# RWKV chunks: every second pair of heads changes sides, and four products use four quarters of the array

## Chip, cores and metric

One core of one Trainium2 chip. The metric is the device time of one launch in microseconds (us), the median of the runs.

## The reference, cut to what matters

The kernel computes a two-block model over 512 tokens of width 1024. The change is inside one branch of the first block, RWKV-7: 16 heads of width 64, each with a 64x64 state that is carried over the tokens.

```python
def step(state, inp):
    r_t, w_t, k_t, v_t, kk_t, b_t = inp
    sk = jnp.einsum('bhvk,bhk->bhv', state, kk_t)
    state = (state * w_t[:, :, None, :] - sk[..., None] * b_t[:, :, None, :]
             + v_t[..., None] * k_t[:, :, None, :])
    return state, jnp.einsum('bhvk,bhk->bhv', state, r_t)
```

## The kernel before, in words

The recurrence is run in 8 chunks of 64 tokens. A chunk needs, per head, the inverse of a triangular 64x64 matrix, which is built up by doubling in five levels, and then a few 64x64 products with the state. Two heads make a pair `j` (8 pairs). Head `i=0` of a pair lives in partitions 0 to 63, head `i=1` in partitions 64 to 127. A 64x64 product takes one quarter of the 128x128 array: its rows are the partitions its operands come from, its columns the partitions of PSUM it writes. Before, nearly all products of head 0 go from rows 0-63 to columns 0-63, those of head 1 from rows 64-127 to columns 64-127, so two quarters on the diagonal are used. Only U writes to the other half of the partitions, and so uses the other two quarters.

**prep(c, blk)** inverts for chunk `c` and four pairs (`blk` 0 or 1, 8 heads):
- gram (L758), transposes bt and vt (L767, L771), the first X product (L777). VectorE makes the masked matrices (L2363, L2366), the first `Xi` (L2376) and the first `Xj` (L2379); ScalarE copies NCc (L1546), BT (L1551) and UV (L1557, key vt); GpSimd makes the masks of each level (L3302).
- then for each level `l` = 1 to 5: P (L786) from `Xj`; ScalarE copies it out to `P1` (L1564, key p1); X (L793) and, below level 5, Y (L798) use P1 and `Xi`. VectorE subtracts Y from `Xj` (L2388, key xj), which is what the next P waits for, and then X from `Xi` (L2392, key xi).

**seq(c)** does the part that depends on the state: R (L813 and, from chunk 1, L816), which ScalarE copies to RS (L1431); U (L824), which ScalarE writes negated into UV (L1577, two instructions, key uv); S (L832) and O (L838, L841), with the new state on VectorE (L2405, L2411) and the output on ScalarE (L1582).

`chunk_turns` (L609) sets the order on every engine: seq(c) in three parts, with seven steps of prep(c+1) for the two blocks in turn after the first and after the second part, and the rest of prep(c+1) behind. In steady state TensorE's order is: R; gram, bt, vt and first X of both blocks; PA(1) (A is block 0, B is block 1, in brackets stands the level); U; PB(1); XA YA XB YB of level 1; PA(2) PB(2) XA YA XB YB of level 2; S and O; PA(3) PB(3) XA YA XB YB; the same for level 4; PA PB XA XB of level 5; R of the next chunk.

PSUM results come from a ring of seven banks (`PS`, class `Ring`). `take` hands out the next bank, and `bank` makes TensorE wait until the bank's previous owner was read out (`prior`). Order and waits on an engine are in program order: what stands behind a wait waits too.

```python
def bank(*key, hold=False):
    b = PS.take(*key, hold=hold)
    for s in due("pe", *PS.prior(*key)):
        pe.wait_ge(*s)
    return b
```

Of the kernel before, what the change touches and what calls it, by code (L numbers as in the profile page):

```python
# [16 lines left out]
S = 512  # L17
# [155 lines left out]
class Ring:  # L173
# [10 lines left out]
    def take(self, *key, hold=False):  # L184
        while self.n % len(self.slots) in self.held:
            self.n += 1
        i = self.n % len(self.slots)
        self.n += 1
        assert key not in self.at, key
        self.at[key], self.before[key], self.owner[i] = i, self.owner[i], key  # L190
        if hold:
            self.held.add(i)
        return self.slots[i]

    def let(self, *key):
        self.held.discard(self.at[key])
# [3 lines left out]

    def prior(self, *key):

        k = self.before[key]
        if k is None:
            return self.after
        return [] if self.known is None else self.known[1][k]

    def free(self, key, *done):
        assert key not in self.freed, key
# [115 lines left out]
def build(nc, T, known=None):  # L325

    with ExitStack() as ctx:
# [36 lines left out]
            return list(zip(tiles(sb(c, name + "h", n * S, dt=F32R)), tiles(sb(c, name + "l", n * S, dt=F32R))))  # L364


        PS = ring("ps", [ctx.enter_context(nc.psum_tensor("ps%d" % i, [128, S], F32))[:, :] for i in range(7)])
        PL = ctx.enter_context(nc.psum_tensor("psl", [128, S], F32))[:, :]
        PT, CT, DP, X = sb(ctx, "PT", NPAR), sb(ctx, "CT", NCON), sb(ctx, "DP", 76), sb(ctx, "X", 8 * S)
        W = Weights(T, sb(ctx, "wraw", NRAW * SLOT), sb(ctx, "whi", NSPL * SLOT, dt=F32R),  # L370
# [138 lines left out]

        halves = [(i, 64 * i, slice(64 * i, 64 * i + 64)) for i in range(2)]  # L510
        each = [(j, i, lo, sl) for j in range(8) for i, lo, sl in halves]
        o3 = YS.rearrange("p (j t) -> p j t", j=8)
        xw, rt, rec, Lc, Pp, Pi, at_, km = Yt

# [105 lines left out]
        def tensor_program(pe):  # L620

            def bank(*key, hold=False):
                b = PS.take(*key, hold=hold)
                for s in due("pe", *PS.prior(*key)):
                    pe.wait_ge(*s)
                return b

            def proj(b, key, w, rhs, hk, c0=0, m=128, start=True, stop=True, k0=0, ks=None):

# [117 lines left out]
            def prep(c, blk):  # L747
                u = c % 2
                cols = slice(256 * blk, 256 * blk + 256)
                xi3, xj3, p13 = (r3(a[:, cols], 64) for a in (Xis[u], Xj, P1))  # L750
                nls = [r3(x[:, cols], 64) for x in NLr]
                mine = [(jj, i, lo, sl) for jj in range(4) for i, lo, sl in halves]
                for s in due("pe", ("dve", "bk", 4 * blk + 3), ("act", "kr", 4 * blk + 3)):
                    pe.wait_ge(*s)
                gram = [r3(bank("gram", c, blk, i), 128) for i in range(2)]
                for jj, i, lo, sl in mine:
                    j = 4 * blk + jj
                    ins = MM(gram[i][:, jj, :], BK5[sl, j, c, :, :].rearrange("p s t -> p (s t)"),  # L758
                             KR5[sl, j, c, :, :].rearrange("p s t -> p (s t)"), start=True, stop=True)
                    if jj == 3:  # L760
                        ins.then_inc(*up("pe", "gram", c, blk, i))
                if c == 0 and blk == 1:
                    rk_sum(7)
                yield
                b3 = r3(bank("bt", c, blk), 128)
                for jj in range(4):
                    ins = TR(b3[:, jj, :], BK5[:, 4 * blk + jj, c, :, :].rearrange("p s t -> p (s t)"), C("ident"))  # L767
                ins.then_inc(*up("pe", "bt", c, blk))
                b3 = r3(bank("vt", c, blk), 128)
                for jj in range(4):  # L770
                    ins = TR(b3[:, jj, :], VFt[4 * blk + jj][:, c // 2 * 128:c // 2 * 128 + 128], C("ident"))  # L771
                ins.then_inc(*up("pe", "vt", c, blk))
                b3 = r3(bank("x", c, blk, 0)[:, 0:256], 64)
                for s in due("pe", ("dve", "lvl", c, blk, 0)):
                    pe.wait_ge(*s)
                for jj, i, lo, sl in mine:
                    ins = MM(b3[sl, jj, :], nls[0][sl, jj, :], C("x0")[sl, :], start=True, stop=True)  # L777
                ins.then_inc(*up("pe", "x", c, blk, 0))
                yield
                yield  # L780
                for l in range(1, 6):
                    b3 = r3(bank("p", c, blk, l)[:, 0:256], 64)
                    for s in due("pe", ("dve", "xj", c, blk, l - 1), ("pool", "lvl", c, blk, l)):
                        pe.wait_ge(*s)
                    for jj, i, lo, sl in mine:
                        ins = MM(b3[sl, jj, :], nls[l % 3][sl, jj, :], xj3[sl, jj, :], start=True, stop=True)  # L786
                    ins.then_inc(*up("pe", "p", c, blk, l))
                    yield
                    b3 = r3(bank("x", c, blk, l)[:, 0:256], 64)
                    for s in due("pe", ("act", "p1", c, blk, l), ("dve", "xi", c, blk, l - 1)):  # L790
                        pe.wait_ge(*s)
                    for jj, i, lo, sl in mine:
                        ins = MM(b3[sl, jj, :], p13[sl, jj, :], xi3[sl, jj, :], start=True, stop=True)  # L793
                    ins.then_inc(*up("pe", "x", c, blk, l))
                    if l < 5:
                        b3 = r3(bank("y", c, blk, l)[:, 0:256], 64)
                        for jj, i, lo, sl in mine:
                            ins = MM(b3[sl, jj, :], xi3[sl, jj, :], p13[sl, jj, :], start=True, stop=True)  # L798
                        ins.then_inc(*up("pe", "y", c, blk, l))
                    yield  # L800


            def seq(c):
                u = c % 2
                GT, BT, UV = GTs[u], BTs[u], UVs[u]
                xi3, rs3, st3 = r3(Xis[u], 64), r3(RS, 64), r3(ST, 64)
                b3 = r3(bank("R", c), 64)
                for blk in range(2):
                    for s in due("pe", ("dve", "gt", c, blk, 1), ("act", "vt", c, blk, 1), ("act", "bt", c, blk),
                                 ("dve", "xi", c, blk, 5), ("dve", "st", c - 1) if c else None):  # L810
                        pe.wait_ge(*s)
                for j, i, lo, sl in each:
                    ins = MM(b3[sl, j, :], GT[sl, j, i, 0:64], UV[sl, j, i, :], start=(j == 0), stop=(c == 0 and j == 7))  # L813
                if c:
                    for j, i, lo, sl in each:
                        ins = MM(b3[sl, j, :], KR5[sl, j, c, 0, :], st3[sl, j, :], start=False, stop=(j == 7))  # L816
                ins.then_inc(*up("pe", "R", c))
                yield
                b3 = r3(bank("U", c), 64)
                for s in due("pe", ("act", "rs", c)):  # L820
                    pe.wait_ge(*s)
                for j, i, lo, sl in each:
                    ul = slice(64 - lo, 128 - lo)
                    ins = MM(b3[ul, j, :], xi3[sl, j, :], rs3[sl, j, :], start=True, stop=True)  # L824
                ins.then_inc(*up("pe", "U", c))
                yield
                if c < 7:
# [585 lines left out]
        def scalar_program(act):  # L1413
# [118 lines left out]
            def prep(c, blk):  # L1532
# [28 lines left out]
                for l in range(1, 6):  # L1561
                    for need in due("act", ("pe", "p", c, blk, l)):
                        act.wait_ge(*need)
                    ACTV(P1[:, cols], PS.of("p", c, blk, l)[:, 0:256], ACT.Copy).then_inc(*up("act", "p1", c, blk, l))  # L1564
                    PS.free(("p", c, blk, l), ("act", "p1", c, blk, l))
                    yield
                    yield

            def seq(c):
                evac(("R", c), RS, ACT.Copy, ("rs", c))  # L1570
                yield
                b3 = r3(PS.of("U", c), 64)
                for need in due("act", ("pe", "U", c)):
                    act.wait_ge(*need)
                for i, lo, sl in halves:
                    ul = slice(64 - lo, 128 - lo)
                    ACTV(UVs[c % 2][ul, :, i, :], b3[ul, :, :], ACT.Copy, scale=-1.0).then_inc(*up("act", "uv", c, i))  # L1577
                PS.free(("U", c), ("act", "uv", c, 1))
                yield
                for need in due("act", ("pe", "O", c)):  # L1580
                    act.wait_ge(*need)
                ACTV(o3[:, :, c * 64:(c + 1) * 64], r3(PS.of("O", c), 64), ACT.Copy).then_inc(*up("act", "o", c))  # L1582
                PS.free(("O", c), ("act", "o", c))
# [571 lines left out]
        def vector_program(dve):  # L2155
# [196 lines left out]
            def prep(c, blk):  # L2352
# [20 lines left out]
                yield  # L2373
                for need in due("dve", ("dve", "lvl", c, blk, 0)):
                    dve.wait_ge(*need)
                TT(xi3, bmid(C("x0"), 4), nl3, SUB).then_inc(*up("dve", "xi", c, blk, 0))  # L2376
                for need in due("dve", ("pe", "x", c, blk, 0), ("pe", "p", c - 1, blk, 5) if c else None):
                    dve.wait_ge(*need)
                TT(xj3, bmid(C("x0"), 4), r3(PS.of("x", c, blk, 0)[:, 0:256], 64),  # L2379
# [3 lines left out]
                for l in range(1, 6):  # L2383
                    yield
                    if l < 5:
                        for need in due("dve", ("pe", "y", c, blk, l), ("dve", "xj", c, blk, l - 1)):
                            dve.wait_ge(*need)
                        TT(Xjb, Xjb, PS.of("y", c, blk, l)[:, 0:256], SUB).then_inc(*up("dve", "xj", c, blk, l))  # L2388
                        PS.free(("y", c, blk, l), ("dve", "xj", c, blk, l))
                    for need in due("dve", ("pe", "x", c, blk, l), ("dve", "xi", c, blk, l - 1)):  # L2390
                        dve.wait_ge(*need)
# [1118 lines left out]
```

## Time and profile before

| | |
|---|---|
| median of 3 runs | 3808.95 us (3808.34 to 3809.26) |
| the profiled execution | 3807.86 us, of which the span is 3806.1 us |
| TensorE busy in the span | 3685.7 us (97%) |
| VectorE, ScalarE busy | 2143.5 us (56%), 1490.1 us (39%) |
| mean granted TensorE clock | 0.984 of 2.4 GHz |
| the chunk stage | about 199.6 to 425 us of the span |

Times in rows are microseconds from the start of the span. TensorE's matmul records are PE, its weight loads PEld. One 64x64 fp32 product shows as two matmul records: the 8 products of P for one block are "x16". A row of the timeline gives start, length from first start to last end, engine, line, operation and count; in square brackets stands how long the engine had been idle and what ended that.

### The profile page before, as it was taken

Reading aid. Unit: us, or ns where it says so; the run is one execution under the profiler, and the core shown is the slowest. Engines: PE = TensorE matmul, PEld = TensorE weight load, DVE = VectorE, ACT = ScalarE, POOL = GpSimd, SP = SyncE. Lnnn points to the kernel's source line nnn. Section 1 sums busy time; section 2 is a strip of 40 time slices with the busy share of each in tenths; the row PEclk is TensorE's granted clock in tenths of the full one; section 3 lists DMA queues with packets and bytes.
Section 4 is the critical chain, followed back from the end, with each engine's and each line's share of the span. In section 5 each row is a group of like instructions: output and inputs, shape, how many; then the busy total and the mean of one; then the engine's idle time right before and its main releaser. Section 6 shows DMA issues by size and latency. Waiting matters only on the chain.

```text
span 3806.1 us, 51932 instructions
## 1 busy us (share of the span) xinstructions
PE 3685.7 (97%) x22058; PEld 2987.6 (78%) x22058; DVE 2143.5 (56%) x3227; ACT 1490.1 (39%) x2593; POOL 72.2 (2%) x92
## 2 busy tenths in 40 slices
PE   8989999899999999999999999999999999999998
PEld 6678688787876887887777888888877778888886
DVE  6865645757444466567575445434665654454346
ACT  5733334335222344343355323223434562332233
POOL 0022000000000000000000000000000000000000
PEclk9999999899999999999999999999999999999999
DMA  3200123022331222323200223232332003332322
GB/s 140 66 3 4 57 89 105 23 100 72 101 115 50 89 95 90 104 89 110 81 1 21 82 95 110 89 106 85 98 107 68 1 23 100 102 105 86 108 87 81
DMA packets 91532, 298.57 MB, mean 78 GB/s; under 512 B 10147, under 2 KB 12707, under 8 KB 90788
## 3 DMA queue, kind: packets, MB, share of 16 engines
q1 hardware_dynamic: 88848, 286.50, 23.2%
q10 hardware_dynamic: 2452, 8.76, 0.6%
q8 instruction: 173, 2.83, 0.3%
q14 instruction: 59, 0.48, 0.0%
HBM read 292.07 MB, written 2.10 MB: 77 GB/s over the span
## 4 chain that ended last, share of the span: by engine, by line
PE 85%; DVE 9%; ACT 4%; issue 1%; DMA 0%; SPq 0%; DVEq 0%; POOL 0%; ACTq 0%; POOLq 0%
PE ps L638 22%; PE ps L640 22%; PE ps L639 22%; PE ps L1264 2%; PE ps L1274 1%; PE psl L1283 1%; DVE wlo L2161 1%; PE ps L1283 1%; ACT whi L1421 1%; PE ps L793 1%; PE ps L677 1%; DVE ftm L2177 1%; PE ps L679 1%; PE ps L678 1%; PE ps L798 1%
## 5 line engine op out<-in xcount | busy, mean ns | idle before, releaser
L2161 DVE TENSOR_TENSOR wlo<-wraw,whi 128x1024 fp32r<-128x1024 f32 (+5 forms) x603 | 663.5, 1102 | 1212.8 <-ACT whi L1421 1203.6
L1421 ACT ACTIVATE whi<-wraw 128x1024 fp32r<-128x1024 f32 (+5 forms) x603 | 576.1, 958 | 1195.3 <-PE ps L640 1117.8
L638 PE MATMUL ps<-HH,whi 128*128 128x512 f32 x1880 | 749.1, 398 | 9.8 <-DVE wlo L2161 7.3
L640 PE MATMUL ps<-HH,wlo 128*128 128x512 f32 x1880 | 733.2, 390 | 0.0
L639 PE MATMUL ps<-HL,whi 128*128 128x512 f32 x1880 | 733.1, 390 | 0.0
L638 PEld LDWEIGHTS ps<-HH,whi 128*128 128x128 f32 x1880 | 353.8, 188 | 98.1 <-issue 12.7
L639 PEld LDWEIGHTS ps<-HL,whi 128*128 128x128 f32 x1880 | 353.9, 188 | 78.8 <-issue 7.5
L640 PEld LDWEIGHTS ps<-HH,wlo 128*128 128x128 f32 x1880 | 353.6, 188 | 74.3
L638 PE MATMUL ps<-HBh,whi 128*128 128x512 f32 x816 | 320.9, 393 | 1.4 <-DVE HBl L2779 0.9
L640 PE MATMUL ps<-HBh,wlo 128*128 128x512 f32 x816 | 317.7, 389 | 0.0
L639 PE MATMUL ps<-HBl,whi 128*128 128x512 f32 x816 | 317.6, 389 | 0.0
L638 PEld LDWEIGHTS ps<-HBh,whi 128*128 128x128 f32 x816 | 153.2, 188 | 35.8 <-DVE HBl L2779 2.1
L639 PEld LDWEIGHTS ps<-HBl,whi 128*128 128x128 f32 x816 | 153.2, 188 | 32.5 <-issue 1.4
L640 PEld LDWEIGHTS ps<-HBh,wlo 128*128 128x128 f32 x816 | 153.2, 188 | 31.9
L638 PE MATMUL ps<-act2h,whi 128*128 128x512 f32 x384 | 149.8, 390 | 0.0
L639 PE MATMUL ps<-act2l,whi 128*128 128x512 f32 x384 | 149.4, 389 | 0.0
L640 PE MATMUL ps<-act2h,wlo 128*128 128x512 f32 x384 | 149.4, 389 | 0.0
L3063 DVE TENSOR_REDUCE sm<-ps 128x1 f32<-128x256 f32 (+3 forms) x192 | 81.2, 451 | 55.5 <-PE ps L1266 55.2
L638 PE MATMUL ps<-yph,whi 128*128 128x512 f32 x256 | 100.2, 391 | 0.7 <-DVE ypl L2170 0.7
L639 PE MATMUL ps<-ypl,whi 128*128 128x512 f32 x256 | 99.6, 389 | 0.0
L640 PE MATMUL ps<-yph,wlo 128*128 128x512 f32 x256 | 99.6, 389 | 0.0
L638 PEld LDWEIGHTS ps<-act2h,whi 128*128 128x128 f32 x384 | 72.1, 188 | 15.8 <-DVE act2l L2170 1.0
(648 smaller groups left out, 6093.5 us busy)
## 6 DMA issues: line engine op xcount, KB each, us to landing
wraw<-in_w_ff SPq DMA_DIRECT2D x88, 512.0 KB, 3.4
wraw<-in_w_bg SPq DMA_DIRECT2D x48, 512.0 KB, 3.4
wraw<-in_ffn_up SPq DMA_DIRECT2D x44, 512.0 KB, 3.2
wraw<-in_w_z SPq DMA_DIRECT2D x36, 512.0 KB, 3.2
wraw<-in_w_gate SPq DMA_DIRECT2D x32, 512.0 KB, 3.3
wraw<-in_w_br SPq DMA_DIRECT2D x32, 512.0 KB, 3.2
wraw<-in_w_rw SPq DMA_DIRECT2D x26, 512.0 KB, 3.3
wraw<-in_w_mam SPq DMA_DIRECT2D x24, 512.0 KB, 3.2
```

What stands on the lines that cost most here:

```text
L638: MM(b[0:m, :], hi[:, k, c0:c0 + m], x[0], start=(start and k == 0), stop=False)
L639: MM(b[0:m, :], hi[:, k, c0:c0 + m], x[1], start=False, stop=False)
L640: ins = MM(b[0:m, :], lo[:, k, c0:c0 + m], x[0], start=False, stop=(stop and k == n - 1))
L677: MM(b[:, 0:cols], x[0][:, cs], hi[:, k, 0:cols], start=first, stop=False)
L678: MM(b[:, 0:cols], x[1][:, cs], hi[:, k, 0:cols], start=False, stop=False)
L679: ins = MM(b[:, 0:cols], x[0][:, cs], lo[:, k, 0:cols], start=False, stop=end)
L793: ins = MM(b3[sl, jj, :], p13[sl, jj, :], xi3[sl, jj, :], start=True, stop=True)
L1264: MM(b[h][:, 0:nk], job["q"](h)[:, qs], job["k"](h)[:, k0:k0 + nk], start=True, stop=False)
L1283: ins = MM(ob[:, 64 * h:64 * h + 64], job["pt"][i % 3][:, 128 * kb:128 * kb + 128], job["v"](h, kb), start=(kb == 0), stop=(kb == nkb - 1))
L1421: ACTV(W.pair_of(n)[0], W.raw_of(n), ACT.Copy).then_inc(*up("act", "whi", n))
L2161: TT(l, W.raw_of(n), h.bitcast(F32), SUB).then_inc(*up("dve", "wlo", n))
L3063: RED(s[:, h:h + 1], PS.of("sc", *key)[:, 0:job["nk"]], AXX, ALU.max, negate=True).then_inc(*(up("dve") if x else up("dve", "mx", *key)))
```

## The change

Every odd pair of heads changes sides on its way. `turned(j, lo)` gives the other half for odd `j`. P of an odd pair is written to the opposite half of PSUM, so that `P1` of that pair lies in the other half; `Xi` of odd pairs lies in the other half too, which the first `Xi` brings about: one VectorE instruction over 128x256 becomes one over 128x128 and two over 64x128. X then reads and writes in the other half (still on the diagonal), Y, R and U go between halves as needed. P, Y, R and U thus use all four quarters, and write even pairs to one bank and odd pairs to another: each takes two neighbouring banks. `Ring.take_two` hands out banks 0-1, 2-3 or 4-5, passing over a bank where it stands on an odd one or on the last (number 6). X, S, O, gram and the transposes take one bank as before; the seven banks stay seven. ScalarE's and VectorE's reads of the four products go over both banks in one instruction.

```diff
+    def take_two(self, *key):
+        n = len(self.slots)
+        while self.n % n % 2 or self.n % n == n - 1 or {self.n % n, self.n % n + 1} & self.held:
+            self.n += 1
+        i = self.n % n
+        self.n += 2
+        assert key not in self.at, key
+        self.at[key], self.before[key] = i, self.owner[i:i + 2]
+        self.owner[i:i + 2] = [key, key]
+        return self.slots[i:i + 2]
...
-        k = self.before[key]
-        if k is None:
-            return self.after
-        return [] if self.known is None else self.known[1][k]
+        done = []
+        for k in self.before[key]:
+            if k is None:
+                done += self.after
+            elif self.known is not None:
+                done += self.known[1][k]
+        return done
...
-        PS = ring("ps", [ctx.enter_context(nc.psum_tensor("ps%d" % i, [128, S], F32))[:, :] for i in range(7)])
+        PSW = [ctx.enter_context(nc.psum_tensor("ps%d" % i, [128, 2 * S if i < 3 else S], F32))[:, :] for i in range(4)]
+        PS = ring("ps", [b for w in PSW for b in tiles(w)])
+
+        def two(key, n):
+
+            w = PSW[PS.at.get(key, 0) // 2 if known is None else known["rings"]["ps"][0][key] // 2]
+            return w.rearrange("p (e n) -> p e n", e=2)[:, :, 0:64 * n].rearrange("p e (a t) -> p e a t", a=n)
+
+        def by_two(ap):
+            return ap.rearrange("p (a e) t -> p e a t", e=2)
...
+        def turned(j, lo):
+            lo = 64 - lo if j % 2 else lo
+            return slice(lo, lo + 64)
...
+            def two_banks(*key):
+
+                banks = [r3(b, 64) for b in PS.take_two(*key)]
+                for s in due("pe", *PS.prior(*key)):
+                    pe.wait_ge(*s)
+                return banks
...
-                    b3 = r3(bank("p", c, blk, l)[:, 0:256], 64)
+                    bb = two_banks("p", c, blk, l)
                     for s in due("pe", ("dve", "xj", c, blk, l - 1), ("pool", "lvl", c, blk, l)):
                         pe.wait_ge(*s)
                     for jj, i, lo, sl in mine:
-                        ins = MM(b3[sl, jj, :], nls[l % 3][sl, jj, :], xj3[sl, jj, :], start=True, stop=True)
+                        ins = MM(bb[jj % 2][turned(jj, lo), jj // 2, :], nls[l % 3][sl, jj, :], xj3[sl, jj, :],
+                                 start=True, stop=True)
                     ins.then_inc(*up("pe", "p", c, blk, l))
                     yield
                     b3 = r3(bank("x", c, blk, l)[:, 0:256], 64)
                     for s in due("pe", ("act", "p1", c, blk, l), ("dve", "xi", c, blk, l - 1)):
                         pe.wait_ge(*s)
                     for jj, i, lo, sl in mine:
-                        ins = MM(b3[sl, jj, :], p13[sl, jj, :], xi3[sl, jj, :], start=True, stop=True)
+                        tl = turned(jj, lo)
+                        ins = MM(b3[tl, jj, :], p13[tl, jj, :], xi3[tl, jj, :], start=True, stop=True)
                     ins.then_inc(*up("pe", "x", c, blk, l))
                     if l < 5:
-                        b3 = r3(bank("y", c, blk, l)[:, 0:256], 64)
+                        bb = two_banks("y", c, blk, l)
                         for jj, i, lo, sl in mine:
-                            ins = MM(b3[sl, jj, :], xi3[sl, jj, :], p13[sl, jj, :], start=True, stop=True)
+                            tl = turned(jj, lo)
+                            ins = MM(bb[jj % 2][sl, jj // 2, :], xi3[tl, jj, :], p13[tl, jj, :], start=True, stop=True)
                         ins.then_inc(*up("pe", "y", c, blk, l))
...
-                b3 = r3(bank("R", c), 64)
+                bb = two_banks("R", c)
                 for blk in range(2):
                     for s in due("pe", ("dve", "gt", c, blk, 1), ("act", "vt", c, blk, 1), ("act", "bt", c, blk),
                                  ("dve", "xi", c, blk, 5), ("dve", "st", c - 1) if c else None):
                         pe.wait_ge(*s)
                 for j, i, lo, sl in each:
-                    ins = MM(b3[sl, j, :], GT[sl, j, i, 0:64], UV[sl, j, i, :], start=(j == 0), stop=(c == 0 and j == 7))
+                    ins = MM(bb[j % 2][turned(j, lo), j // 2, :], GT[sl, j, i, 0:64], UV[sl, j, i, :], start=(j < 2),
+                             stop=(c == 0 and j > 5))
                 if c:
                     for j, i, lo, sl in each:
-                        ins = MM(b3[sl, j, :], KR5[sl, j, c, 0, :], st3[sl, j, :], start=False, stop=(j == 7))
+                        ins = MM(bb[j % 2][turned(j, lo), j // 2, :], KR5[sl, j, c, 0, :], st3[sl, j, :], start=False,
+                                 stop=(j > 5))
                 ins.then_inc(*up("pe", "R", c))
                 yield
-                b3 = r3(bank("U", c), 64)
+                bb = two_banks("U", c)
                 for s in due("pe", ("act", "rs", c)):
                     pe.wait_ge(*s)
                 for j, i, lo, sl in each:
-                    ul = slice(64 - lo, 128 - lo)
-                    ins = MM(b3[ul, j, :], xi3[sl, j, :], rs3[sl, j, :], start=True, stop=True)
+                    ul, tl = slice(64 - lo, 128 - lo), turned(j, lo)
+                    ins = MM(bb[j % 2][ul, j // 2, :], xi3[tl, j, :], rs3[tl, j, :], start=True, stop=True)
                 ins.then_inc(*up("pe", "U", c))
...
-                    ACTV(P1[:, cols], PS.of("p", c, blk, l)[:, 0:256], ACT.Copy).then_inc(*up("act", "p1", c, blk, l))
+                    ACTV(by_two(r3(P1[:, cols], 64)), two(("p", c, blk, l), 2), ACT.Copy).then_inc(*up("act", "p1", c, blk, l))
...
-                    ACTV(UVs[c % 2][ul, :, i, :], b3[ul, :, :], ACT.Copy, scale=-1.0).then_inc(*up("act", "uv", c, i))
+                    ACTV(by_two(UVs[c % 2][:, :, i, :])[ul], b4[ul], ACT.Copy, scale=-1.0).then_inc(*up("act", "uv", c, i))
...
-                TT(xi3, bmid(C("x0"), 4), nl3, SUB).then_inc(*up("dve", "xi", c, blk, 0))
+                TT(xi3[:, 0::2, :], bmid(C("x0"), 2), nl3[:, 0::2, :], SUB)
+                for i, l_, sl in halves:
+                    ins = TT(xi3[turned(1, l_), 1::2, :], bmid(C("x0")[sl, :], 2), nl3[sl, 1::2, :], SUB)
+                ins.then_inc(*up("dve", "xi", c, blk, 0))
...
-                        TT(Xjb, Xjb, PS.of("y", c, blk, l)[:, 0:256], SUB).then_inc(*up("dve", "xj", c, blk, l))
+                        TT(by_two(xj3), by_two(xj3), two(("y", c, blk, l), 2), SUB).then_inc(*up("dve", "xj", c, blk, l))
```

## Rows read from the trace of the kernel before

**Rows 1.** Windows of the chunk stage: stretch, its length, busy time (and records) by engine, clock, DMA.
```profile
195.00:420.00 225.00, 203.20 (x5586) 186.90 (x5586) 120.92 (x264) 80.55 (x193) 57.56 (x80) 0.98 0.03 8
```

**Rows 2.** Groups by line in that stage: busy us, mean ns | idle before.
```profile
L793 PE MATMUL ps<-Xi,P 64*64 64x64 f32 x1280 | 51.8, 220 | 2.5 <-ACT P L1564 2.1
...
L786 PE MATMUL ps<-Xj,NL 64*64 64x64 f32 x1280 | 51.5, 221 | 2.3 <-POOL NL L3302 0.3 <-DVE Xj L2388 0.2
...
L798 PE MATMUL ps<-P,Xi 64*64 64x64 f32 x1024 | 40.5, 218 | 0.0
...
L813 PE MATMUL ps<-UV,X 64*64 64x64 f32 x256 | 9.2, 220 | 4.9 <-DVE Xi L2392 4.9
...
L824 PE MATMUL ps<-RSs,Xi 64*64 64x64 f32 x256 | 9.2, 221 | 0.7 <-ACT RSs L1431 0.7
...
L816 PE MATMUL ps<-ST,KR 64*64 64x64 f32 x224 | 7.9, 218 | 0.0
```

**Rows 3.** Timeline of one chunk, where its four stretches begin.
```profile
249.03 1.15 PE L813 MATMUL ps<-UV,X 64*64 64x64 f32 x32 [0.61 <-DVE Xi L2392]
...
257.38 0.51 PE L786 MATMUL ps<-Xj,NL 64*64 64x64 f32 x10
...
267.54 1.10 PE L786 MATMUL ps<-Xj,NL 64*64 64x64 f32 x32
...
276.82 1.15 PE L813 MATMUL ps<-UV,X 64*64 64x64 f32 x32 [0.62 <-DVE Xi L2392]
```

**Rows 4.** Timeline of one level, from P of level 4 to P of level 5.
```profile
270.60 1.37 PE L786 MATMUL ps<-Xj,NL 64*64 64x64 f32 x32
...
271.15 0.41 DVE L2392 TENSOR_TENSOR Xi<-Xi,ps 128x256 f32<-128x256 f32 x1
...
271.28 0.38 ACT L1564 ACTIVATE P<-ps 128x256 f32<-128x256 f32 x1 [2.20 <-PE ps L786]
...
271.80 0.63 PE L793 MATMUL ps<-Xi,P 64*64 64x64 f32 x16
...
273.67 1.37 PE L786 MATMUL ps<-Xj,NL 64*64 64x64 f32 x32
```

**Rows 5.** Chain that ended last, same level.
```profile
270.81 0.43 DVE Xj L2388
...
271.24 0.04 issue
```

**Rows 6.** Timeline where P and U stand beside each other.
```profile
257.68 0.27 PE L824 MATMUL ps<-RSs,Xi 64*64 64x64 f32 x2
...
257.69 0.28 PE L786 MATMUL ps<-Xj,NL 64*64 64x64 f32 x3
...
258.50 0.27 PE L786 MATMUL ps<-Xj,NL 64*64 64x64 f32 x2
...
258.54 0.28 PE L824 MATMUL ps<-RSs,Xi 64*64 64x64 f32 x3
```

**Rows 7.** Timeline of VectorE and ScalarE around the first P.
```profile
256.53 0.42 DVE L2376 TENSOR_TENSOR Xi<-CT,NL 128x256 f32<-128x256 f32 x1
...
257.20 0.91 DVE L2376 TENSOR_TENSOR Xi<-CT,NL 128x256 f32<-128x256 f32 x1
...
257.55 0.77 ACT L1557 ACTIVATE UV<-ps 64x256 f32<-64x256 f32 x2
...
258.87 1.21 ACT L1577 ACTIVATE UV<-ps 64x512 f32<-64x512 f32 x2
```

**Rows 8.** Windows with the granted clock, and one row at the lower clock.
```profile
255.00:258.00 3.00, 2.06 (x49) 1.71 (x49) 2.97 (x6) 2.76 (x8) 2.21 (x4) 1.00 0.00 0
...
415.00:420.00 5.00, 3.54 (x108) 3.15 (x102) 0.50 (x2) 0.71 (x2) 0.00 (x0) 1.00 0.00 0
...
420.00:425.00 5.00, 3.72 (x64) 3.47 (x64) 0.00 (x0) 1.15 (x3) 0.00 (x0) 0.66 0.01 3
...
421.15 1.97 PE L838 MATMUL ps<-X,UV 128*64 128x64 f32 x32 [1.31 <-ACT UV L1577]
```

More of the change, by code:

```diff
@@ L189, in take @@
         assert key not in self.at, key
-        self.at[key], self.before[key], self.owner[i] = i, self.owner[i], key
+        self.at[key], self.before[key], self.owner[i] = i, [self.owner[i]], key
         if hold:
@@ L1569, in seq @@
             def seq(c):
-                evac(("R", c), RS, ACT.Copy, ("rs", c))
+                for need in due("act", ("pe", "R", c)):
+                    act.wait_ge(*need)
+                ACTV(by_two(r3(RS, 64)), two(("R", c), 4), ACT.Copy).then_inc(*up("act", "rs", c))
+                PS.free(("R", c), ("act", "rs", c))
                 yield
-                b3 = r3(PS.of("U", c), 64)
+                b4 = two(("U", c), 4)
                 for need in due("act", ("pe", "U", c)):
```

## The prediction

> **What bounds the kernel now.** I read the windows first: over the chunk stage TensorE is busy 203 of 225 us, VectorE 121, ScalarE 81, at nearly the full clock [rows 1]. TensorE looks like the bound. The groups say what fills it: P, X and Y in 3584 records, R and U in 736 [rows 2]. Then the timeline of one level. XA, YA, XB, YB start at 271.80 and the next P at 273.67 [rows 4]: 64 records in 1.87 us, so 29.2 ns from record to record, while one record lasts 220 ns [rows 2]; records overlap, and it is the rate that counts. A level takes 273.67 - 270.60 = 3.07 us [rows 4], of which 96 records at 29.2 ns make 2.80. The rest is PB waiting for its `Xj`: YB is through at 270.60, VectorE starts at 270.81, so 0.21 later, takes 0.43, and 0.04 of issue follow before PB at 271.28 [rows 4, 5]. The copy of PA starts as far behind it: PA's 16 records are through at 271.07, the copy starts at 271.28 and takes 0.38 [rows 4]; the 0.05 behind a copy I take like the 0.04 behind VectorE. So behind the busy share stand two chains, one per block, nearly as long as the work: P, 0.21, copy 0.38, 0.05, X, Y, 0.21, xj 0.43, 0.04. (A and B are blocks 0 and 1; a number in brackets is the level.)
>
> **What four quarters free.** With two quarters, each takes a record every 58 ns. With four, one every 14.6 ns in all, if the streams don't hinder each other. No single product does that now, but two do side by side: U uses the other two quarters, and where it meets P both run at their own pace: three records of P in 0.28 and three of U in 0.28 [rows 6], less the 0.22 of one record 0.06 for two steps, 30 ns each. P of block 1 starts at 258.50 while records of U, which stand ahead of it in the program, start at 258.54 [rows 6]. So the array takes records of other quarters past waiting ones. I take 14.6 ns; the other end is 29.2. A rule speaks against this: the Trainium skill, "TensorE: Matmul & The Clock Gate", section "The mechanism", says that matmuls start and end strictly in program order. By that rule the sum would be that of the second rival below; the trace of P and U disagrees with it.
> P 1280 records, Y 1024, R 480 and U 256 [rows 2] save 3040 x 14.6 ns = 44 us of TensorE's work. How much of it comes through, I work out by the four stretches of a cycle [rows 3], which is 27.79 us long (276.82 - 249.03).
>
> **What takes it back: the banks.** A level took 6 banks out of 7; now it takes 10, and pairs only at even places. Writing the ring out gives this, the same in every chunk from level 3 on: PA [0,1], PB [2,3] or PA [2,3], PB [4,5]; XA in 4 or 6, YA [0,1], XB in 2, YB [4,5]. Three waits are new and bind. YB of levels 2 and 4 takes the bank of XA of the same level, which is free only after VectorE's xj and xi of block 0. PB of levels 2, 4 and 5 takes the bank of XB of the level before, so it waits for xi of block 1 and not only for xj. U takes the banks of bt and vt of block 1, so it waits for ScalarE's vt. Behind each of them waits all of TensorE's queue: behind YB the next PA, behind PB the next XA, though the copy of PA is long there, behind U the PB of level 1.
> In the walks below, each time is that of the latest thing waited for. 16 records take 0.47 on two quarters and 0.23 on four; a reader starts 0.21 after the last of them was issued; from the start of xj to that of xi are 0.34, xi takes 0.41, a copy 0.38 [rows 4, 5], and 0.05 pass before TensorE goes on.
>
> **Stretch 1, R to gram.** 64 records at half the step: -0.93. Nothing covers it: gram, and behind it VectorE, follow at once.
> **Stretch 2, gram to PA(1).** VectorE sets the pace here, and the first Xi becomes three instructions. One of 256 columns takes 0.42 [rows 7] and lets the next start 0.34 later. If the step scaled with width, three of 128 would take 0.51 (+0.17); if not at all, 1.02 (+0.68). On ScalarE a 256-wide copy takes 0.38 [rows 4] and a 512-wide one 0.60 [rows 7], so some 0.16 doesn't scale; with that I take 0.62: +0.28. The same for block 1, where the row shows 0.91 beside GpSimd [rows 7], falls where TensorE waits for ScalarE (next) and costs nothing; without that cover +0.3 to +0.6.
> **Stretch 3, PA(1) to PA(3),** 10.16 before [rows 3]. From PA(1): vt ends at 258.32 [rows 7], now 0.66 after PA; U 0.71 to 1.18, uv (1.21 for two [rows 7]) 1.39 to 2.60, the copy of PB to 2.90, XB 2.95, YB to 3.65, PA(2) to 3.88, xj 3.86, xi 4.20 to 4.61, PB(2) 4.66 to 4.89, XA to 5.36, YA to 5.59, XB to 6.06; YB waits: xj 5.80, xi 6.14 to 6.55; YB 6.60 to 6.83. S and O are unchanged, 96 records of 29.2 ns and some 0.2 where the shape of the products changes: 3.0. PA(3) at 9.8: -0.34.
> **Stretch 4, PA(3) to R,** 9.28 before. ScalarE copies O first, so XA(3) starts at 0.21 + 0.60 + 0.38 + 0.05, less some 0.1 for the overlap of two copies: 1.14, as before, since P is over by then either way; YB ends at 2.54; PA(4); xj 2.75, xi 3.09 to 3.50; PB(4) 3.55, XA 3.78, YA to 4.48; xj 4.69, xi 5.03 to 5.44; YB 5.49, PA(5) to 5.95; xi of block 1 to 6.69, PB(5) 6.73, XA 6.97; XB 7.61 to 8.08, xi to 8.71, R 8.85: -0.43. With no bank waits it would be 1.2 less.
> ScalarE's and VectorE's reads over two banks I cost at nothing (same elements, one instruction); SyncE's loads of x behind O of chunks 6 and 7 keep their place, the weight loads are far ahead.
>
> **Sum.** A full cycle: -0.93 + 0.28 - 0.34 - 0.43 = -1.42, seven of them -9.9. The preparation of chunk 0 has both waits at every level: 3.19 for 3.07 four times, and Xi: +0.8. R of chunk 0 is half as long: +0.5. The last R and U: -0.9 and -0.5. In all -10.0 of the 44 freed. Against the profiled execution's 3807.86 that is 3797.9; the median lies 1.1 above it: 3799.
>
> **Rivals.**
> *The clock falls.* Less work per time means more idle stretches. Where TensorE was busy 2.06 of 3.00 us the clock stayed at 2.4 GHz; after 3.54 of 5.00, most of the idle time in its second half, it was at 1.2 for part of the next stretch (0.66 in the mean) [rows 8]. Around PA(1) it will be busy some 1.9 of 3.4 (the same stretch with 0.3 more to wait and with PA and U shorter, an estimate), between the two. At 1.2 GHz 32 records took 1.97 [rows 8], so (1.97 - 0.27)/31 = 55 ns each, not 29; with chains beside it, 1.0 to 1.7 us per fall of 3.4 us. Once per chunk: 3807 to 3812. Chance 0.14.
> *No four-quarter rate within one product.* Each product is two records on the same quarter, and if the second holds up what follows, two records per 58 ns stay, as now. This is the case on the other side; its place is YB and PB behind the new bank waits. Per cycle: YB of levels 2 and 4 +0.54 each (xi ends 1.90 after XA's start, XB at 1.40), PB of levels 2, 4 and 5 +0.33 each, U's wait +0.36, Xi +0.28: +2.7, times seven and 3.8 for chunk 0: +23, 3832. On a line between -10 at 14.6 ns and +23 at 29.2 the gain is gone at a step of 19 ns, and from 22 ns on it is slower by over 0.2%. For it: the two records. Against it: rows 6. Chance 0.12. By the Trainium skill's rule of program order ("TensorE: Matmul & The Clock Gate", "The mechanism") this would be the outcome.
> *The waits bind less,* because read-outs come sooner than I chain them. Without any of them a cycle gains the 1.2 of stretch 4 and 0.9 in stretch 3 (PB(2) 0.33, YB(2) 0.54): 2.1, times seven, 3784. Against it: each length is from a row. Chance 0.08.
> *The change doesn't do what it says:* X keeps two quarters, as the diff says; nothing else in it can fail quietly.
>
> **Numbers.** My forecast, 3799 with its own range 3794 to 3807 (step 14.6 to 17 ns, Xi +0.17 to +0.68 a chunk), has 0.66. Range over all: 3788 to 3813, leaving out most of the second and third rival. 0.2%, 7.6 us, is about what can be told from no change: faster means under 3801.3. From the forecast 0.46 of its 0.66 lies there, with the third rival 0.54; within 0.2%: 0.20 and 0.09 of the clock's case, 0.29; slower 0.17.
>
> **What would show it.** P and Y of 16 records should last about 0.45 in place of 0.63, R's 64 about 1.15, at an unchanged 218 ns per record. TensorE's busy time should fall far more than the span, and idle time stand ahead of L793, L798 and L786 with VectorE's L2392 as what ended it. Xi of the first level shows three instructions. Levels 3.07 long should become 2.3 to 3.2, in turns. The granted clock in the stage should stay at 0.98. Wrong: P of 16 still at 0.63 (no four quarters), a clock under 0.95 in the stage, or a cycle under 26 or over 27.

## The result, and the profile after

The change makes the kernel slower: 3817.5 us against 3809.0, medians of 11 runs each, ratio 1.0024 with an interval of 1.0016 to 1.0031. 3799 was predicted. The profiled execution took 3814.36 us with a span of 3812.6, 6.5 longer than before. The runs further down were measured at other times, and each is compared with the kernel before as measured beside it (medians of 3807.4 to 3810.1), so differences between runs are best read from their ratios.

First the windows of the chunk stage after the change (stretch, length, busy time and records of TensorE, weight loads, VectorE, ScalarE, GpSimd; granted clock, DMA):

```profile
215.00:400.00 185.00, 142.31 (x4624) 127.87 (x4624) 102.72 (x233) 63.37 (x151) 43.38 (x60) 0.95 0.01 3
290.00:295.00 5.00, 3.70 (x105) 3.52 (x108) 2.26 (x6) 1.95 (x4) 2.79 (x5) 0.66 0.01 3
318.00:322.00 4.00, 3.50 (x106) 3.31 (x108) 1.83 (x6) 1.83 (x4) 3.07 (x5) 0.57 0.02 6
376.00:384.00 8.00, 6.56 (x196) 6.10 (x187) 3.27 (x9) 2.72 (x6) 3.93 (x6) 0.57 0.02 4
```

In the same 185 us before, TensorE was busy 170.3 us at a clock of 1.00. Now it is 142.3 at 0.95, and the clock is at its lower level (1.2 GHz) for a part of five of the six full cycles. Each such drop and return is called a fall below. The groups answer to [rows 2]:

```profile
L831 PE MATMUL ps<-Xi,P 64*64 64x64 f32 x1280 | 56.4, 231 | 4.4 <-ACT P L1605 4.0
...
L822 PE MATMUL ps<-Xj,NL 64*64 64x64 f32 x1280 | 37.6, 237 | 28.9 <-DVE Xi L2439 14.8 <-DVE Xj L2426 11.5 <-issue 1.9
L837 PE MATMUL ps<-P,Xi 64*64 64x64 f32 x1024 | 34.8, 240 | 7.0 <-DVE Xi L2439 7.0
...
L2422 DVE TENSOR_TENSOR Xi<-CT,NL 64x128 f32<-64x128 f32 x32 | 16.9, 528 | 0.4
```

P is busy 37.6 us where it was 51.5, but TensorE now stands idle 28.9 us ahead of it, where it was 2.3. Two things end that idle time: the read-out of X (L2439), which frees a bank, and the first Xj (L2426). The timeline of a level answers to [rows 4]; it runs from PB(4) to PB(5):

```profile
275.02 0.46 PE L822 MATMUL ps<-Xj,NL 64*64 64x64 f32 x16 [0.57 <-DVE Xi L2439]
275.30 0.57 PE L831 MATMUL ps<-Xi,P 64*64 64x64 f32 x14
...
276.00 0.67 PE L831 MATMUL ps<-Xi,P 64*64 64x64 f32 x16
276.25 0.42 DVE L2435 TENSOR_TENSOR Xj<-Xj,ps 128x256 f32<-128x256 f32 x1 [1.28 <-PE ps L837]
276.59 0.41 DVE L2439 TENSOR_TENSOR Xi<-Xi,ps 128x256 f32<-128x256 f32 x1
277.06 0.46 PE L837 MATMUL ps<-P,Xi 64*64 64x64 f32 x16 [0.39 <-DVE Xi L2439]
277.34 0.41 PE L822 MATMUL ps<-Xj,NL 64*64 64x64 f32 x16
277.59 0.42 DVE L2435 TENSOR_TENSOR Xj<-Xj,ps 128x256 f32<-128x256 f32 x1 [0.58 <-PE ps L837]
...
277.92 0.42 DVE L2439 TENSOR_TENSOR Xi<-Xi,ps 128x256 f32<-128x256 f32 x1
278.40 0.46 PE L822 MATMUL ps<-Xj,NL 64*64 64x64 f32 x16 [0.64 <-DVE Xi L2439]
```

P and Y of 16 records take 0.46 in place of 0.63, for which this is a row of the kernel before:

```profile
259.48 0.63 PE L798 MATMUL ps<-P,Xi 64*64 64x64 f32 x16
```

So four quarters work at the full rate. The waits stand where they were written out: YB(4) at 277.06 and PB(5) at 278.40, each behind an `Xi` update. The first P of a chunk is the other place (before in [rows 7]):

```profile
259.31 0.28 DVE L2420 TENSOR_TENSOR Xi<-CT,NL 128x128 f32<-128x128 f32 x1
...
259.60 1.14 DVE L2422 TENSOR_TENSOR Xi<-CT,NL 64x128 f32<-64x128 f32 x2
...
260.78 0.42 DVE L2426 TENSOR_TENSOR Xj<-CT,ps 128x256 f32<-128x256 f32 x1
261.12 0.37 DVE L2420 TENSOR_TENSOR Xi<-CT,NL 128x128 f32<-128x128 f32 x1
261.25 0.46 PE L822 MATMUL ps<-Xj,NL 64*64 64x64 f32 x16 [1.24 <-DVE Xj L2426]
261.49 1.02 DVE L2422 TENSOR_TENSOR Xi<-CT,NL 64x128 f32<-64x128 f32 x2
...
262.55 0.42 DVE L2426 TENSOR_TENSOR Xj<-CT,ps 128x256 f32<-128x256 f32 x1
263.02 0.46 PE L822 MATMUL ps<-Xj,NL 64*64 64x64 f32 x16 [0.84 <-DVE Xj L2426]
```

The three instructions of Xi take 1.47 us from start to Xj's start, where one took 0.34, and TensorE waits 1.24 for PA(1) and 0.84 for PB(1). Chunks 4 and 6 are like this one. In chunks 3, 5 and 7 the three for block 0 take 0.91 and those for block 1 take 1.86 (before, the one took 0.33 for block 0 and 0.83 to 0.87 for block 1).

The table takes the starts of R, PA(1), PA(3) and the next R from each kernel's timeline, for the six full cycles (from chunk 1 on), and sums from the first P to the last R of the stage. It is the ruler for all that follows.

| us | R to PA(1) | PA(1) to PA(3) | PA(3) to R | cycle | first P to R of chunk 0 | R of chunk 0 to R of chunk 7 |
|---|---|---|---|---|---|---|
| before | 8.35 | 10.16-10.22 | 9.28 | 27.8 | 15.9 | 193.2 |
| change | 7.97-8.53 | 9.94-12.00 | 9.47 | 27.9-30.0 | 18.1 | 200.5 |
| e1 bank plan | 7.97-8.60 | 9.55-11.25 | 8.37-9.09 | 25.9-28.2 | 14.9 | 188.1 |
| e2 Xj first | 7.06-7.17 | 10.80-10.87 | 9.47-9.72 | 27.3-27.6 | 17.1 | 192.2 |
| e3 banks alone | 8.30 | 11.91-12.08 | 10.62-10.76 | 30.8-31.0 | 19.7 | 215.1 |
| e4 Xi in three | 8.83 | 10.70 | 9.28 | 28.8 | 18.6 | 200.2 |
| e5 plan, Xj first | 7.06-7.17 | 9.64-10.85 | 8.37-9.09 | 25.2-26.7 | 14.7 | 180.5 |
| e9 GpSimd waits | 7.97 | 9.93-11.11 | 9.47-9.72 | 27.4-28.7 | 17.5 | 193.7 |

The 6.5 us of the span come out as +2.3 before R of chunk 0, +7.3 in the seven cycles, +0.7 ahead of the first P, and -3.7 from the last R to the end: R and U are shorter there, and the clock, low at L838 before [rows 8], stays up.

### The profile page after: what moved, and what is told of

Same layout as the page of the kernel before. It is cut to its first block, busy times and chain, and to the rows that moved or that the text cites. A ratio compares the mean times of both kernels' runs of the same rounds, so it can differ in the third digit from the quotient of the medians.

```text
span 3812.6 us, 51930 instructions
## 1 busy us (share of the span) xinstructions
PE 3655.9 (96%) x22058; PEld 2953.9 (77%) x22058; DVE 2157.4 (57%) x3259; ACT 1490.0 (39%) x2593; POOL 72.5 (2%) x92
## 4 chain that ended last, share of the span: by engine, by line
PE 83%; DVE 12%; ACT 4%; issue 2%; DMA 0%; SPq 0%; DVEq 0%; ACTq 0%
PE ps L674 22%; PE ps L676 22%; PE ps L675 22%; PE ps L1305 2%; DVE wlo L2205 2%; PE ps L1315 1%; PE psl L1324 1%; ACT whi L1462 1%; PE ps L1324 1%; PE ps L713 1%; DVE ftm L2221 1%; PE ps L715 1%; PE ps L714 1%; PE ps L831 1%; PE ps L1236 1%
## 5 line engine op out<-in xcount | busy, mean ns | idle before, releaser
L674 PEld LDWEIGHTS ps<-act2h,whi 128*128 128x128 f32 x384 | 72.1, 188 | 15.9 <-DVE act2l L2214 0.9
```

What stands on the lines that cost most here:

```text
L674: MM(b[0:m, :], hi[:, k, c0:c0 + m], x[0], start=(start and k == 0), stop=False)
```

## The experiments

**e1, a bank plan in place of the ring.** No P, X or Y waits for a bank any more: PA and YA in banks 0-1, PB and YB in 2-3, X in 4 and 5 (6 at level 3). `place` records the previous owners as `take_two` does; all seven banks now belong to one PSUM tensor.

```diff
+        def spot(kind, c, blk=0, l=0):
+            if kind == "gram":
+                return 2 + 2 * blk + l
+            if kind in ("bt", "vt"):
+                return {"bt": (6, 2), "vt": (0, 3)}[kind][blk]
+            if kind == "x":
+                return (1, 4)[blk] if l == 0 else (6 if l == 3 else 4, 5)[blk]
+            if kind in ("p", "y"):
+                return 2 * blk
+            return {"R": 0, "U": 5, "S": 6, "O": 4}[kind]
...
-                banks = [r3(b, 64) for b in PS.take_two(*key)]
+                banks = [r3(b, 64) for b in PS.place(spot(*key), 2, *key)]
```

> The changed kernel with a bank plan written out in place of the ring: P and Y of block 0 always in banks 0-1, of block 1 in 2-3, X in 4 and 5 (6 at level 3), U in 5-6, so that no P, X or Y waits for a bank. If the bank waits are what takes the gain back, levels go from 3.35 and 2.80 us to about 2.3, the stretch from P of level 3 to R from 9.47 to about 8.3, and the time falls by 15 to 20 us to 3797 to 3802 (less if the clock falls more often, as the stage gets emptier). If the waits are only another face of the chain of copies, levels stay over 3 us and the time within 3 us of 3817.

Measured: 3801.1 us, ratio to the kernel before 0.9984 (0.9974 to 0.9993). The levels of chunk 0 take 2.47 to 2.52 where they took 3.37; PA(3) to R is 8.37 in most cycles, 8.3 expected. What a P waits for is now its own Xj, and shorter:

```profile
288.01 0.46 PE L844 MATMUL ps<-Xj,NL 64*64 64x64 f32 x16 [0.31 <-DVE Xj L2457]
```

The first P of block 1 is put down to ScalarE's UV in the list of waits (7 times), but it starts 0.10 us behind the end of its Xj in all seven, so that its wait too is for its input. The clock still falls (mean 0.95 from 215 to 400 us), once each in two full cycles, of 28.1 and 28.2 against 25.9 to 27.2. The change lies 8.6 us over the kernel before, this one 6.5 under it: the bank waits are a cause, worth 15 us of time.

**e3, the banks without the gain.** The two-bank ring with no head turned and Xi in one instruction: `turned` returns the same half, all else as in the change.

```diff
         def turned(j, lo):
-            lo = 64 - lo if j % 2 else lo
             return slice(lo, lo + 64)
...
-                TT(xi3[:, 0::2, :], bmid(C("x0"), 2), nl3[:, 0::2, :], SUB)
-                for i, l_, sl in halves:
-                    ins = TT(xi3[turned(1, l_), 1::2, :], bmid(C("x0")[sl, :], 2), nl3[sl, 1::2, :], SUB)
-                ins.then_inc(*up("dve", "xi", c, blk, 0))
+                TT(xi3, bmid(C("x0"), 4), nl3, SUB).then_inc(*up("dve", "xi", c, blk, 0))
```

> The kernel with two banks for each P, Y, R and U and the same ring of seven as in the change, but with no head turned: two quarters as before, the first Xi in one instruction. If the array's rate and the banks are separate terms, this pays for the banks without the gain: levels of 3.1 to 4.0 us, 20 us over the kernel before, about 3829. If the waits are hidden at the slower rate, 3809.

Measured: 3834.1 us, ratio 1.0072 (1.0057 to 1.0087).

```profile
332.70 0.68 PE L821 MATMUL ps<-Xj,NL 64*64 64x64 f32 x16 [0.38 <-DVE Xi L2435]
...
335.17 0.68 PE L836 MATMUL ps<-P,Xi 64*64 64x64 f32 x16 [0.39 <-DVE Xi L2435]
```

P and Y last 0.68 and wait for the same two read-outs as in the change. Pairs of banks in a ring of seven cost 26 us by themselves (25 by the two profiled spans), with the clock at 1.00 from 215 to 400 us.

**e4, Xi in three, alone.** The kernel before with three instructions, on the same halves:

```diff
-                TT(xi3, bmid(C("x0"), 4), nl3, SUB).then_inc(*up("dve", "xi", c, blk, 0))
+                TT(xi3[:, 0::2, :], bmid(C("x0"), 2), nl3[:, 0::2, :], SUB)
+                for i, l_, sl in halves:
+                    ins = TT(xi3[sl, 1::2, :], bmid(C("x0")[sl, :], 2), nl3[sl, 1::2, :], SUB)
+                ins.then_inc(*up("dve", "xi", c, blk, 0))
```

> The kernel before with only the first Xi in three instructions (same halves). If three instructions beside GpSimd are what holds up the first P, it comes 0.5 to 1.1 us later in each chunk; some of it hides under ScalarE's copies of U, so the time rises by 2 to 8 us, to 3811 to 3817. The clock should not fall in the stage except at its end, since the rest of the stage is as full as before. If the pieces cost what their width says, under 2 us.

Measured: 3816.1 us, ratio 1.0024 (1.0015 to 1.0034), as much as the whole change costs. Every cycle is 1.0 longer, half of it ahead of PA(1), half behind it. The second part I had taken to be hidden under ScalarE's copies of U. It isn't: PB(1) waits for its Xj, and XA behind PB. The profiled execution is one of the longer ones (3818.2), and in it the clock fell once in chunk 0 (near 210 us), which I had not expected; so a part of the 8.5 us can be the clock's.

**e9, GpSimd kept away from Xi.** The change, with one wait more on GpSimd:

```diff
+                if blk:
+                    for need in due("pool", ("dve", "xi", c, blk, 0)):
+                        pool.wait_ge(*need)
                 level(1)
                 level(2)
```

> The changed kernel with GpSimd made to wait, ahead of its level masks of block 1, until the first Xi of block 1 is made, so that these three VectorE instructions have no GpSimd work beside them. If GpSimd beside them is what stretches them, each takes 0.28 us and the three some 0.7 to 0.85 in a row (0.37 and 1.0 to 1.45 in the change), and Xj of block 1 comes sooner. If they are long for their shape, they stay over 1.3. The first P of block 1 then waits for its mask, 0.75 us, so the time moves little, 3814 to 3820.

Measured: 3810.7 us, ratio 1.0001 (0.9992 to 1.0011), better than expected. Groups of lines of this kernel:

```profile
L2422 DVE TENSOR_TENSOR Xi<-CT,NL 64x128 f32<-64x128 f32 x32 | 9.6, 300 | 0.4
L2420 DVE TENSOR_TENSOR Xi<-CT,NL 128x128 f32<-128x128 f32 x16 | 4.6, 290 | 0.0
```

In the change the first of these groups took 528 ns in the mean, here 300. So it is GpSimd's masks beside them, not the shape, that stretch the instructions. The excess over the kernel before went from 8.6 us to 0.6, so that one added wait took 8 us off. More than half of it is the clock's: between R of chunk 0 and R of chunk 7 a single fall is left where the change had five, one of them twice as long as the others, and full cycles without a fall take 27.4 to 27.6, against 27.9 in the change. The Trainium skill, "SBUF — State Buffer", section "Who interferes with whom", says that a VectorE instruction with two inputs in SBUF contends with a GpSimd instruction that reads SBUF. The trace agrees: Xi has both inputs in SBUF; Xj (L2426), which reads one from PSUM, takes 422 ns in the change and 410 before.

**e2, Xj ahead of Xi.** The change, with the Xj block moved ahead of the three instructions; P needs only Xj.

```diff
-                TT(xi3[:, 0::2, :], bmid(C("x0"), 2), nl3[:, 0::2, :], SUB)
-                for i, l_, sl in halves:
-                    ins = TT(xi3[turned(1, l_), 1::2, :], bmid(C("x0")[sl, :], 2), nl3[sl, 1::2, :], SUB)
-                ins.then_inc(*up("dve", "xi", c, blk, 0))
                 for need in due("dve", ("pe", "x", c, blk, 0), ("pe", "p", c - 1, blk, 5) if c else None):
                     dve.wait_ge(*need)
                 TT(xj3, bmid(C("x0"), 4), r3(PS.of("x", c, blk, 0)[:, 0:256], 64),
                    SUB).then_inc(*up("dve", "xj", c, blk, 0))
                 PS.free(("x", c, blk, 0), ("dve", "xj", c, blk, 0))
+                TT(xi3[:, 0::2, :], bmid(C("x0"), 2), nl3[:, 0::2, :], SUB)
+                for i, l_, sl in halves:
+                    ins = TT(xi3[turned(1, l_), 1::2, :], bmid(C("x0")[sl, :], 2), nl3[sl, 1::2, :], SUB)
+                ins.then_inc(*up("dve", "xi", c, blk, 0))
```

> The changed kernel with one move: the first Xj is made ahead of the three instructions for the first Xi. If these stand in the way of the first P, the first P comes 0.5 to 1.1 us sooner in a chunk for block 0 and about 2 us sooner for block 1, X of level 1 is then held by Xi or by ScalarE, and the time falls by 4 to 10 us. If Xi is hidden, nothing changes.

Measured: 3806.5 us, ratio 1.0000 (0.9991 to 1.0009), 9 to 10 us less than the change when each is held against its kernel before, the top of the expected gain. PA(1) comes 0.8 to 1.5 us sooner after R than in the change. The next wait shows the third bank wait of the prediction, U behind ScalarE's vt:

```profile
314.97 0.69 PE L865 MATMUL ps<-RSs,Xi 64*64 64x64 f32 x32 [0.89 <-ACT UV L1598]
```

In the six full cycles the clock stays up here, and all of them lie between 27.3 and 27.6. So, as in e9, a good part of the gain lies in falls that are gone and not in the shorter wait itself.

**e8, the same order in the kernel before.**

```diff
-                TT(xi3, bmid(C("x0"), 4), nl3, SUB).then_inc(*up("dve", "xi", c, blk, 0))
...
                 PS.free(("x", c, blk, 0), ("dve", "xj", c, blk, 0))
+                TT(xi3, bmid(C("x0"), 4), nl3, SUB).then_inc(*up("dve", "xi", c, blk, 0))
```

> The kernel before with only the first Xj ahead of the first Xi. The first P comes 0.3 us sooner; if nothing else holds it, the time is 2 to 3 us shorter (3805 to 3807), which would be within what a measurement tells from no change. If the gain of the last two runs comes from this order and not from the four quarters, it is 8 us or more.

Measured: 3807.3 us, ratio 0.9998 (0.9990 to 1.0007): no difference. PA(1) is 0.15 to 0.3 sooner after R, and PA(3) 0.17 later behind it. So the order is worth nothing in the kernel before, where Xi is one instruction, and the gain of e2 is not one of the order alone.

**e7, filler products against the fall of the clock.** In the change, 12 products on the spare bank behind the first X of block 1 and 12 behind U.

```diff
+            def fill(n):
+                for s in due("pe", ("dve", "bs")):
+                    pe.wait_ge(*s)
+                for k in range(n):
+                    sl = slice(64 * (k % 2), 64 * (k % 2) + 64)
+                    ins = MM(PL[sl, 0:64], C("x0")[sl, :], C("x0")[sl, :], start=True, stop=True)
+                ins.then_inc(*up("pe"))
...
                 ins.then_inc(*up("pe", "x", c, blk, 0))
+                if c and blk == 1:
+                    fill(12)
...
                 ins.then_inc(*up("pe", "U", c))
+                if c < 7:
+                    fill(12)
```

> The changed kernel with 12 filler products behind the first X of block 1 and 12 behind U, in TensorE's idle time; nobody reads them. If the falls of the clock cost some 7 us in the stage, the clock stays at its upper level between 203 and 420 us, the stretch from the first P to P of level 3 is 9.9 us in every chunk (it is 9.94 to 12.0), and the time is 3809 to 3812. If the long stretches have another cause, they stay with the clock up, at 3817.

Measured: 3812.5 us, ratio 1.0013 (1.0004 to 1.0022), against 1.0024 for the change; the two intervals overlap. The clock stays up from 219 to 420 us, and the seven cycles take 197.4 in place of 200.5. But two of them are long with the clock up (28.4 and 28.5; PA(1) to PA(3) takes 9.9 to 11.1, not 9.9 in every chunk as expected), so that the fillers get in the way somewhere, or something else stretches these; and the clock falls in chunk 0 and once near 423. The profiled execution is also the longest of the ten, 3819.6. The run speaks for the clock without settling its size. Better are the kernels in which single cycles differ by a fall: in e9 five cycles take 27.4 to 27.6, and the one with a fall in it 28.7; in e2, without any, all are alike. A fall costs 1.1 to 1.2 us. Two rows of windows, 215 to 400 us, of e2 and then of the filler run:

```profile
215.00:400.00 185.00, 143.32 (x4748) 127.85 (x4750) 111.13 (x246) 68.47 (x164) 46.82 (x67) 0.99 0.01 3
```

```profile
215.00:400.00 185.00, 148.75 (x4983) 134.25 (x4984) 104.19 (x236) 63.97 (x152) 44.38 (x62) 0.99 0.02 4
```

TensorE is busy hardly more in e2 than in the change (143.3 and 142.3), and the clock still holds. What differs between the two is the idle time ahead of PA(1) and PB(1), which is shorter in e2; the kernels don't show more than that of the cause of a fall.

**e5 and e11, plan and order together.** The edits of e1 and e2 in one kernel, run in two jobs.

> The bank plan and the first Xj ahead of Xi together. If the two were separate terms of the loss, the cycle of a chunk gets under 26 us (from 27.9 to 30.0), levels of chunk 0 stay at 2.5, and the time comes to 3788 to 3795. If the gain of one only opens the wait of the other, it stays near the 3801 of the bank plan alone.

> The bank plan and Xj ahead of Xi once more, beside the run before it on the same chip: 3787 to 3792.

Measured: 3790.3 us, ratio 0.9955 (0.9942 to 0.9969), and again 3792.1, ratio 0.9959 (0.9945 to 0.9972). This beats both kernels, by 17 and 27 us. The full cycles take 25.2 to 26.7 in e5, so not all are under 26 as expected. What P (L844) waits for in e5, by the list of waits:

```profile
PE ps L844 <- DVE Xj L2444: 8.8, 7, 1.3
PE ps L844 <- DVE Xj L2457: 6.6, 23, 0.7
```

No wait for an Xi update is left among the P and Y (14.8 and 7.0 us in the change); the two that remain are the true inputs of P.

**e6, the same with 8 fillers behind U.** `fill` as in e7, in e5:

```diff
                 ins.then_inc(*up("pe", "U", c))
+                if c < 7:
+                    fill(8)
```

> The same with 8 filler products behind U, whose results nobody reads, in TensorE's idle time. If the clock falls in the run without them, it stays up here, and the time is 1 to 2 us per saved fall shorter; if no fall is there to save, the two are the same within 3 us.

Measured: 3794.2 us, ratio 0.9960 (0.9948 to 0.9973), the same as without. In the profile the clock stays up all through the stage and the seven cycles take 178.3 in place of 180.5, but that doesn't show in the medians; the profiled execution, 3788.3, is the fastest of its five.

**e10, all three.** The kernel of e5 with the wait of e9, the same three lines ahead of `level(1)`.

> The bank plan, the first Xj ahead of Xi, and GpSimd's wait together. If the three are separate terms, this is the fastest: 3783 to 3789, with cycles of 25 us or less. If GpSimd's wait only moves the mask of block 1 into the chain that Xj has just left, it is no faster than the two alone (3790), or up to 4 us slower.

Measured: 3801.3 us, ratio 0.9980 (0.9971 to 0.9989), so 9 us worse than e11, the same without GpSimd's wait in the same job, and outside both expectations. Once Xj has left the queue behind Xi, the mask of block 1 is what PB(1) waits for (PA(1) to PA(2) takes 4.5 to 4.6 with the clock up, 4.1 to 4.2 in e11), and the clock falls in three of the full cycles (26.9 to 27.3 against 25.7 to 26.1):

```profile
PE ps L844 <- POOL NL L3371: 9.5, 5, 2.1
```

## Why the prediction was wrong

- **The rate of four quarters: right.** 16 records last 0.46, and R took 1.09 in place of 2.01 up to gram: -0.92 for -0.93 predicted. TensorE's busy time fell by 30 us over the span. "No four-quarter rate" fell; as a price of the banks its sum was some 5 us short: +23 computed, of which 2 for Xi, against +26 measured in e3. That 3832 and 3834 lie so near each other is luck, as the kernel before was 1.4 us faster beside e3 and Xi is not in it.
- **The bank waits: right in place, a little short in size.** YB(2), YB(4) and PB(2), PB(4), PB(5) wait as written out. The third wait, U behind ScalarE's vt, hardly bound in the change (its weight loads waited 1.1 us for it in all), as PA(1) came late itself; it shows in e2. Stretch 4 came to 9.47 and not 8.85. PA(3) to PA(4) took 2.80 (2.54), PA(4) to PA(5) 3.35 (3.18), the rest 3.32 (3.13). Two sizes were off: a run of products that starts after a wait goes slower at its start (P is followed by X 0.28 after it began, not 0.23), and XA(3) starts 1.34 behind PA(3), not 1.14. A tenth of that is only the boundary: PA(3) starts ahead of O's last records now. Stretch 3 was -0.22 with the clock up, for -0.34.
- **Xi in three: this step failed.** "I take 0.62: +0.28", with +0.68 as the far end, priced three instructions without GpSimd, and held block 1 for hidden. Alone each piece starts 0.30 after the one before it, so 0.9 for three, since a 64x128 piece takes as long as a 128x128 one (0.28); beside GpSimd it took 1.47 in the rows above. Stretches 1 and 2 came to +0.18 in one cycle of two and to -0.38 in the other, where -0.65 was predicted, and what the latter gains is lost again ahead of PB(1), for which block 1's three take 1.86 (with the clock up, in e7, 10.37 from PA(1) to PA(3) in place of 9.95). e4 puts the whole term at 8.5 us, where some 2 us were in the sum. The row of 0.91 for one instruction against 0.42 [rows 7] had shown the stretching; I read it for block 1 alone and gave it a cover that wasn't there.
- **The clock: a rival at 0.14 that happened.** In five of six full cycles, as "once per chunk" had it, and in the stretch named, around PA(1) and PB(1). The excess of the five over the one undisturbed, 27.94, is 5.8 us, so 1.2 a cycle (1.0 to 1.7 predicted). The reading it went by was wrong: busy 1.9 of 3.4 us does not lie "between the two" rows (2.06 of 3.00 and 3.54 of 5.00) but is less than either. It isn't independent of the step before: where the idle time ahead of PA(1) and PB(1) gets shorter, by the order (e2) or by shorter instructions (e9), the five falls of the full cycles go down to none and to one.
- **The sum.** Against the -10.0 predicted stand three errors: Xi (8.5 in e4 against some 2, +6.5, perhaps with a fall in it), the levels (+0.6 a cycle, and more in chunk 0, so +5) and the falls (+5.8). Their 17 us are most of the 18.5 us between 3799 and 3817.5. They are read from e4 and from the change, so they need not add up exactly. A cycle over 27, which the prediction had named as a sign of being wrong, came in all seven. The bank waits, Xi and the falls together took back all that the 44 us of array work gave; with the bank plan and the first Xj ahead of Xi (e5) the gain is 17 us.

## What to carry to other kernels

When an engine works faster by writing to more banks, count the banks per round against the ring first, and write the ring's owners out: here the same seven banks with a fixed plan turned +8.6 us into -6.5, and a moved instruction made it -17. Price an instruction that is split in pieces from a row with its neighbours beside it: here one of 0.34 us became three of 0.9 together, and 1.4 to 1.9 beside GpSimd. Put what the next stage waits for ahead of it. And where an engine is given less to do, look for the stretch where its new idle time comes together: in this kernel the clock fell there, and stayed up in the full cycles where that wait was taken away (e2).

## What the runs showed that I had not expected

By the trace, records of TensorE do not start in program order across the quarters. In the change PA(3) begins before O's last records, although it stands behind them:

```profile
271.19 0.27 PE L822 MATMUL ps<-Xj,NL 64*64 64x64 f32 x2
271.24 0.23 PE L882 MATMUL ps<-KR,ST 64*64 64x64 f32 x2
```

A wait added on an engine that nobody seemed to wait for (GpSimd, busy 58 us of the stage) took 8 us off one kernel and put 9 us on another (e9, e10). Its sign changed with what stood next in the chain.
